# Gathering the tokens of four experts at a time in a decoder layer's mixture of experts

## The reference

```python
logits = (t @ w_router + b_router).astype(jnp.float32)
top_v, top_i = lax.top_k(logits, TOP_K)
gates = jax.nn.softmax(top_v, axis=-1)
...
gu = xb @ w_gate_up[ei] + b_gate_up[ei]
gate = jnp.minimum(gu[:, :D_FF], SWIGLU_LIMIT)
up = jnp.clip(gu[:, D_FF:], -SWIGLU_LIMIT, SWIGLU_LIMIT)
act = gate * jax.nn.sigmoid(gate * SWIGLU_ALPHA)
return ((up + 1.0) * act) @ w_down[ei] + b_down[ei]
```

## Time and profile before

| what | us |
|---|---|
| median of 3 runs | 1342.67 |
| lowest and highest of them | 1340.54, 1344.32 |
| profiled execution, its time | 1343.27 |
| span of the profiled execution | 1341.4 |
| PE busy in it (94%) | 1260.1 |
| DVE, ACT busy | 315.5, 159.9 |

### The profile page before, as it was taken

How to read it: one execution, slowest core, us unless ns; L and a number is a source line. 1 busy time by engine, 2 the same in 40 slices (tenths; PEclk the granted TensorE clock), 3 DMA queues, 4 the chain that set the end, 5 groups by cost and what they waited for, 6 DMA issues and landing times.

```text
span 1341.4 us, 15435 instructions
## 1 busy us (share of the span) xinstructions
PE 1260.1 (94%) x6339; PEld 606.3 (45%) x6339; DVE 315.5 (24%) x591; ACT 159.9 (12%) x305; POOL 84.5 (6%) x110
## 2 busy tenths in 40 slices
PE   5999999999799999999999999999999999999986
PEld 4757666764533434343443434343443434343431
DVE  2334446442211111122111111121111111121112
ACT  2214322112100001010000001010000001010001
POOL 4176500000000000000000000000000000000000
PEclk9989999989599999999999999999999999999998
DMA  9247570345386999999999999999999999999991
GB/s 316 79 131 245 170 250 1 139 196 184 157 322 260 414 421 414 419 417 417 419 414 422 414 422 414 419 417 417 419 415 422 414 422 414 419 417 417 420 414 43
DMA packets 92203, 447.63 MB, mean 334 GB/s; under 512 B 6282, under 2 KB 15926, under 8 KB 59269
## 3 DMA queue, kind: packets, MB, share of 16 engines
q1 hardware_dynamic: 85495, 427.36, 79.2%
q0 software_dynamic: 5632, 18.88, 4.5%
q10 hardware_dynamic: 1046, 0.97, 0.3%
HBM read 445.74 MB, written 1.68 MB: 334 GB/s over the span
## 4 chain that ended last, share of the span: by engine, by line
PE 76%; DMA 17%; DVE 3%; ACT 2%; issue 1%; SPq 1%; ACTq 0%; DVEq 0%
PE ps L942 19%; PE ps L997 17%; DMA arena<-in_w_gate_up 16%; PE ps L900 11%; PE ps L776 5%; PE ps L749 2%; PE ps L1009 2%; PE ps L605 2%; DVE arena L1642 2%; PE ps L1018 1%; PE ps L492 1%; PE ps L623 1%; PE ps L1014 1%; PE ps L538 1%; PE ps L646 1%
## 5 line engine op out<-in xcount | busy, mean ns | idle before, releaser
L942 PE MATMUL ps<-arena 128*64 128x512 f32 x2048 | 452.5, 597 | 30.8 <-DMA arena<-in_w_gate_up 23.6
L942 PEld LDWEIGHTS ps<-arena 128*64 128x64 f32 x2048 | 155.9, 137 | 315.2 <-issue 314.8
L997 PE MATMUL ps<-arena 128*64 128x512 f32 x1024 | 225.2, 597 | 4.8 <-ACT arena L1043 4.8
L1043 ACT ACTIVATE arena<-ps 128x512 f32<-128x512 f32 (+9 forms) x170 | 96.0, 582 | 532.2 <-PE ps L997 210.8
L900 PE MATMUL ps<-arena 128*128 128x128 f32 (+1 forms) x768 | 142.7, 318 | 1.3 <-DVE arena L1601 1.3
L997 PEld LDWEIGHTS ps<-arena 128*64 128x64 f32 x1024 | 74.4, 138 | 145.1 <-issue 144.6
L900 PEld LDWEIGHTS ps<-arena 128*128 128x128 f32 (+1 forms) x768 | 109.0, 195 | 44.2 <-issue 15.5
L1622 DVE TENSOR_SCALAR arena<-ps 128x512 f32<-128x512 f32 x32 | 22.1, 691 | 420.2 <-PE ps L942 420.2
L1217 ACT ACTIVATE arena<-arena 128x512 f32<-128x512 f32 x32 | 20.2, 630 | 490.1 <-DVE arena L1622 490.1
L1639 DVE TENSOR_TENSOR arena<-arena,ps 64x512 f32<-64x512 f32 x16 | 10.9, 679 | 270.0 <-PE ps L1014 270.0
L776 PE MATMUL ps<-arena 128*128 128x280 f32 x256 | 66.0, 414 | 0.0
(11 more groups left out here) (286 smaller groups left out, 765.9 us busy)
## 6 DMA issues: line engine op xcount, KB each, us to landing
arena<-in_w_gate_up SPq DMA_DIRECT2D x128, 2048.0 KB, 15.5
arena<-in_w_down SPq DMA_DIRECT2D x64, 2048.0 KB, 16.9
arena<-in_w_in SPq DMA_DIRECT2D x8, 1024.0 KB, 9.4
arena<-in_w_out SPq DMA_DIRECT2D x2, 2048.0 KB, 11.7
arena<-in_w_in SPq DMA_DIRECT2D x2, 1088.0 KB, 12.9
arena<-in_w_in SPq DMA_DIRECT2D x1, 2048.0 KB, 23.5
arena<-in_consts SPq DMA_DIRECT2D x1, 1104.0 KB, 8.8
arena<-in_w_uq SPq DMA_DIRECT2D x1, 768.0 KB, 15.8
```

What stands on the lines that cost most here:

```text
L942: m = mm(ps[SL * e:SL * e + SL, b, :], xg[:, 2 * c + kk, SL * e:SL * e + SL], w[e][:, kk, b, :], start=(c == 0 and kk == 0), stop=(c == 3 ...
L997: m = mm(ps[SL * e:SL * e + SL, u, :], hidT[:, 4 * c + kk, SL * e:SL * e + SL], w[e][:, kk, u, :], start=(c == 0 and kk == 0), stop=(c == ...
L1043: return act.activation(out, in_, ACT.Copy)
```

## The change

- `pick` is made for four experts at once (u = 4), once for every two pairs; `xg` holds the gathered rows of four experts (2048 columns in place of 1024). `pick`, `xg` and `pick_bias` change places in the arena.
- Pairs are now even (u = 0) or odd (u = 1). From pair 1 on, PE gathers only in odd pairs, for the two pairs that follow: `gather_four(0)` for the first four blocks of features where `gather` stood, and `gather_four(4)` for the other four behind the transposes of `hid`. Each is 12 matmuls with 256 columns and fills banks 6 and 7; between them ACT copies the banks out (`take_four`). Even pairs have no gather. Pair 0 still gathers for pair 1 alone, with 128 columns.
- `pickg` is still made for each pair (`weigh_pair`); the choice of four runs on DVE early in an even pair, once at the start, and at the end of pair 0.
- The loop's body is two pairs and runs 6 times (pairs 2 to 13); pairs 0, 1, 14 and 15 are written out. SP's code is untouched. In `pair`, the inner index u is renamed v; these lines are left out below.

```diff
@@ -196,16 +197,16 @@
         gates = at(take(NT * NE), NT * NE).rearrange("p (t e) -> p t e", t=NT)
         most = at(take(2), 2)
         most_i = at(take(2), 2).bitcast(I32)
-        pick = at(take(NT * P), NT * P).rearrange("p (t u s) -> p t u s", t=NT, u=2)
+        pick = at(norm2_start + SLOT, NT * 2 * P).rearrange("p (t u s) -> p t u s", t=NT, u=4)
         pickg = at(take(NT * P), NT * P).rearrange("p (t u s) -> p t u s", t=NT, u=2)
         pickT = at(hT0 + 4 * D, NT * P).rearrange("p (t n) -> p t n", t=NT)
-        xg = at(norm2_start + SLOT, KD * P).rearrange("p (k s) -> p k s", k=KD)
+        xg = at(take(KD * 2 * P), KD * 2 * P).rearrange("p (k s) -> p k s", k=KD)
         y_last = at(take(512), 512)[0:64, :]
...
-        pick_bias = at(take(P), P)
+        pick_bias = at(norm2_start + SLOT + 768, P)
         assert 4 * D + NT * P <= 2 * KD * T
...
@@ -891,21 +892,33 @@
 
             pe.sem_inc(pe_comb, 1)
 
-            def gather(count):
+            def gather(count, u):
 
                 pe.wait_ge(pick_ready, count)
                 for k in range(KD):
                     for t in range(NT):
                         n = ROWS[t]
                         m = mm(ps[:, 6 + k // 4, P * (k % 4):P * (k % 4) + P], h2[0:n, t, P * k:P * k + P],
+                               pick[0:n, t, u:u + 2, :].rearrange("p u s -> p (u s)"), start=(t == 0),
+                               stop=(t == NT - 1))
+                m.then_inc(pe_gather, 1)
+
+            def gather_four(k0):
+
+                for k in range(4):
+                    for t in range(NT):
+                        n = ROWS[t]
+                        m = mm(ps[:, 6 + k // 2, 2 * P * (k % 2):2 * P * (k % 2) + 2 * P],
+                               h2[0:n, t, P * (k0 + k):P * (k0 + k) + P],
                                pick[0:n, t, :, :].rearrange("p u s -> p (u s)"), start=(t == 0), stop=(t == NT - 1))
                 m.then_inc(pe_gather, 1)
 
-            def pair(n, extra, ahead, first=False, last=False):
+            def pair(n, extra, ahead, u=0, first=False, last=False):
+
                 if extra:
                     pe.wait_ge(y_added, 3 * n + 1)
-                    gather(n + 1)
-                pe.wait_ge(xg_ready, n + 1)
+                    gather(n - NP + NQ + 1, 0)
+                pe.wait_ge(xg_ready, n + 1 if first or extra or u else n + 2)
 
                 pe.wait_ge(pickg_ready, n + 1)
                 for t in range(NT):
...
                              [(kk, b) for kk in range(2) for b in range(4)])
                     for j, (kk, b) in enumerate(order):
                         for e in range(2):
...
-                            m = mm(ps[SL * e:SL * e + SL, b, :], xg[:, 2 * c + kk, SL * e:SL * e + SL],
+                            m = mm(ps[SL * e:SL * e + SL, b, :], xg[:, 2 * c + kk, P * u + SL * e:P * u + SL * e + SL],
...
+                elif ahead is not None:
+                    pe.wait_ge(pickT_ready, n + 1)
+                    pe.wait_ge(y_added, 3 * n + 1)
+                    pe.wait_ge(pick_ready, ahead)
+                    gather_four(0)
 
...
+                    pe.wait_ge(xg_ready, n + 2)
+                    gather_four(4)
                 for c in range(2):
...
-                    m = mm(ps[32 * u:32 * u + 32, 6, :], pickT[:, 2, 0:32], ye[:, 512 * u:512 * u + 512],
+                if first:
+                    pe.wait_ge(xg_ready, n + 2)
+                elif ahead is not None:
+                    pe.wait_ge(xg_ready, n + 3)
+                for v in range(2):
...
-            with pe.Fori(1, NP - 1) as p:
-                pair(p, False, True)
-            pair(NP - 1, False, False, last=True)
+            gather(1, 0)
+            pair(0, False, None, 0, first=True)
+            pair(1, False, 2, 1)
+            with pe.Fori(1, NQ - 1) as q:
+                pair(2 * q, False, None, 0)
+                pair(2 * q + 1, False, q + 2, 1)
+            pair(NP - 2, False, None, 0)
+            pair(NP - 1, False, None, 1, last=True)
             pe.wait_ge(most_ready, 1)
             count = pe.value_load(most_i[0:1, 0:1], min_val=0, max_val=T)
             with pe.If(count > SL):
...
 
 
-            def take_gathered(count):
+            def take_gathered(count, u):
                 act.wait_ge(pe_gather, count)
-                copy(xg, ps[:, 6:8, :].rearrange("p b (k s) -> p (b k) s", k=4)).then_inc(xg_ready, 1)
...
-
-            def pair(n, extra, ahead, first=False):
+                copy(xg[:, :, P * u:P * u + P], ps[:, 6:8, :].rearrange("p b (k s) -> p (b k) s", k=4)
+                     ).then_inc(xg_ready, 1)
+
+            def take_four(count, k0):
+                act.wait_ge(pe_gather, count)
+                copy(xg[:, k0:k0 + 4, :], ps[:, 6:8, :].rearrange("p b (k s) -> p (b k) s", k=2)).then_inc(xg_ready, 1)
+
+            def pair(n, extra, ahead, u=0, first=False):
...
                     act.activation(sgm[:, half_row], gate[:, half_row], ACT.Sigmoid, scale=ALPHA
                                    ).then_inc(sgm_ready, 1)
+                if ahead and u:
+                    take_four(n + 2, 0)
                 act.wait_ge(pe_hidT, 2 * n + 1)
                 copy(hidT[:, 0:4, :], ps[:, 4, :].rearrange("p (j n) -> p j n", j=4)).then_inc(hidT_act, 1)
-                if ahead:
-                    take_gathered(n + 2)
-                for u in range(2):
-                    if u == 0:
+                if first:
+                    take_gathered(n + 2, 1)
+                elif ahead and u:
+                    take_four(n + 3, 4)
+                for v in range(2):
...
-            def choose(experts, count, first):
-
-                iota = const["iota"][:, first].unsqueeze(1).unsqueeze(1).to_broadcast([P, NT, 2, SL])
-                dve.tensor_tensor(pick, iota, rank[:, :, experts].unsqueeze(3).to_broadcast([P, NT, 2, SL]),
+            def choose(experts, count, first, u=slice(0, 4)):
+
+                m = u.stop - u.start
+                iota = const["iota"][:, first].unsqueeze(1).unsqueeze(1).to_broadcast([P, NT, m, SL])
+                dve.tensor_tensor(pick[:, :, u, :], iota, rank[:, :, experts].unsqueeze(3).to_broadcast([P, NT, m, SL]),
                                   ALU.is_equal).then_inc(pick_ready, 1)
+
+            def weigh_pair(experts, count, u):
+
                 dve.wait_ge(pick_ready, count)
-                dve.tensor_tensor(pickg, pick, gates[:, :, experts].unsqueeze(3).to_broadcast([P, NT, 2, SL]),
+                dve.tensor_tensor(pickg, pick[:, :, u, :], gates[:, :, experts].unsqueeze(3).to_broadcast([P, NT, 2, SL]),
                                   ALU.mult).then_inc(pickg_ready, 1)
 
-            def pair(p, n, extra, first, ahead):
-                if ahead:
-                    dve.wait_ge(pe_gather, n + 1)
-                    dve.wait_ge(pe_pick, n + 1)
-                    choose(bass.ds(2 * p + 2, 2), n + 2, first)
+            def pair(p, n, extra, first, u, q=None, ahead=True):
+
                 if extra:
                     choose_bias(bass.ds(p, 1))
-                    choose(bass.ds(2 * p, 2), n + 1, first)
-
-                for u in range(2):
-                    at_u = slice(512 * u, 512 * u + 512)
-                    if u == 0:
+                    choose(bass.ds(2 * p, 2), n, first, slice(0, 2))
+                    weigh_pair(bass.ds(2 * p, 2), n - NP + NQ + 1, slice(0, 2))
+                elif u == 0:
+                    dve.wait_ge(pe_pick, n + 1)
+                    weigh_pair(bass.ds(2 * p + 2, 2), 1 if q is None else q + 1, slice(2, 4))
+                    if ahead and q is not None:
+                        dve.wait_ge(pe_gather, n + 2)
+                        dve.wait_ge(pickg_ready, n + 2)
+                        choose(bass.ds(2 * p + 4, 4), q + 2, first)
+                elif ahead:
+                    dve.wait_ge(pe_pick, n + 1)
+                    weigh_pair(bass.ds(2 * p + 2, 2), 2 if q is None else q + 2, slice(0, 2))
+
...
+                    dve.wait_ge(up_ready, 4 * n + 2 * v + 2)
+                    dve.wait_ge(sgm_ready, 2 * n + v + 1)
                     dve.tensor_tensor(hid[:, at_u], up[:, at_u], sgm[:, at_u], ALU.mult).then_inc(hid_ready, 1)
...
+                if u == 0 and q is None and not extra:
+                    dve.wait_ge(pe_gather, 2)
+                    choose(slice(4, 8), 2, first)
                 dve.wait_ge(y_added, 3 * n + 3)
...
-            choose(slice(0, 2), 1, slice(0, SL))
+            choose(slice(0, 4), 1, slice(0, SL))
+            weigh_pair(slice(0, 2), 1, slice(0, 2))
...
-            with dve.Fori(0, NP - 1) as p:
-                pair(p, p, False, slice(0, SL), True)
-            pair(NP - 1, NP - 1, False, slice(0, SL), False)
+            pair(0, 0, False, slice(0, SL), 0)
+            pair(1, 1, False, slice(0, SL), 1)
+            with dve.Fori(1, NQ - 1) as q:
+                pair(2 * q, 2 * q, False, slice(0, SL), 0, q)
```

(43 more changed lines are left out.)

47 lines of the change are left out of this document (23 added, 24 removed).

## The result

| | median us | lowest, highest |
|---|---|---|
| before, 5 runs | 1342.67 | 1339.18, 1344.32 |
| changed, 5 runs | 1356.71 | 1355.46, 1362.60 |

The change makes the kernel slower: ratio 1.013, 95% interval 1.0106 to 1.0153, some 14 us. That lies above the forecast's range, which ended at 1350 us. The profiled execution took 1362.6 us, the longest of its five, with a span of 1360.8 us against 1341.4.

What follows compares the result with a forecast made beforehand. The prediction took the loads (DMA) as the bound from pair 2 on, at 60.24 us a pair. 1343.27 + 0.6 for the start + 0 for the end gave 1343.9 us, no change, with range 1340.8 to 1350 us.

Steps and rivals of the forecast that it cites:

- The loads are the bound from pair 2 on: From pair 2 on, loads set 60.24 us a pair; PE has 1.69 us of air, so saving PE work gains nothing.
- Even pairs gain 6.35 us: Even pairs 2 to 14: dropping the 8.51 us gather saves PE 6.35 us, as making `hid` is then exposed.
- Odd pairs: 10.7 us for the wide gather, 11.7 at most: Odd pairs 1 to 13: 48 instructions of 256 columns at 0.222 us, making PE 2.2 us late (2.0 to 3.2).
- The cover is 3.7 us, 2.9 for pair 2: Queued transfers at the queue's thinnest place, said to absorb the odd pair's 2.2 us delay at cost 0.
- The start: +0.6 us: Ahead of the first gather: DVE's choice for 768 elements, not 384, delays it unhidden by 0 to 0.6 us.
- Rival 1: PE falls to half clock behind longer waits in odd pairs; no change, or 1355 us in the longer form; chance 0.11.
- Rival 2: Wide gather: 256 columns cost twice 128 (17.0 us), delaying seven odd pairs; +33 us, 1377 us; chance 0.03.
- Rival 3: The two-pair loop body no longer stays on the core, so PE stands at each turn; 1359 us; chance 0.05.
- Rival 4: In the loop, loads were held back by PE, so 53 us would go, to 1290 us; chance 0.03.

Runs made afterwards that it cites:

- e10: The kernel before, with the third token tile at 128 rows only in the gathers of pairs 1 to 14: 1341.42 us, ratio 0.9999.
- e1: The changed kernel, with the third token tile taken at all 128 rows (zero-padded) in the wide gather: 1346.99 us, ratio 1.0037.
- e3: The changed kernel without the third token tile in the wide gather, so 24 tokens are left out: 1341.34 us, ratio 1.0008.
- e7: The changed kernel, with 128 rows in the wide gather's third tile and a discarded narrow gather in the even pairs: 1343.82 us, ratio 1.0017.
- e2: The changed kernel, with the wide gather's second half moved into the following even pair, ahead of its third gate stage: 1346.16 us, ratio 1.0031.
- e5: The changed kernel, with the wide gather's second half moved into the even pair and 128 rows in the third tile in all gathers: 1331.68 us, ratio 0.9923.
- e6: The kernel before, with 128 rows in the third token tile in all its gathers: 1329.47 us, ratio 0.9905.
- e11: The kernel before, with 128 rows in the third tile only in the first gather and that of pair 0: 1328.93 us, ratio 0.9900.
- e9: The changed kernel, with the wide gather's tiles taken 0, 1, 2 and 2, 1, 0 in turn, the third keeping 24 rows: 1352.34 us, ratio 1.0083.

## Why the prediction was wrong

- *The loads are the bound from pair 2 on.* Right: in e10 41 us less work on TensorE left the time as it was.
- *Even pairs gain 6.35 us.* Right: at 641 us of the changed kernel the transposes wait for `hid` as those of pair 15 did:

```profile
641.40 0.65 PE L983 MATMUL ps<-arena 128*128 128x128 f32 x4 [0.96 <-DVE arena L1674]
643.28 0.66 PE L983 MATMUL ps<-arena 128*128 128x128 f32 x4 [1.23 <-DVE arena L1683]
643.87 7.09 PE L1018 MATMUL ps<-arena 128*64 128x512 f32 x32
```

- *Odd pairs: 10.7 us for the wide gather, 11.7 at most.* **This is the step that failed.** It took 13.5 us, and the odd pair was 4.8 us late, not 2.2, more than the 3.7 us queued. The term left out 16 changes between 128 and 24 rows at 0.17 to 0.20 us, together 2.9 us (13.5 against 10.6 in e1). The rows of 280 columns were nearest in columns but not in rows; with equal tiles they were right to 0.002 us (e1: 0.220 against 0.222 scaled). Rows ahead of the prediction held the hint: 8.51/48 = 0.177 us for 128 columns, where half of the 0.218 us that the down stages give for 256 columns is 0.109. I divided and did not ask where 0.07 us went.
- *The cover is 3.7 us, 2.9 for pair 2.* Right for the loop: at full clock, delays of -1.4 us (e3) and 2.1 (e7) gave no gap there, 4.8 us (changed kernel) gave 0.8 to 1.4. Too large for pair 2: the gap in pair 1 is 0.4 to 0.5 us at a delay of 2.1 (e1, e7) and 2.6 at 4.8, so the cover there was 1.6 to 2.2 us. The delay of 4.8 us was 2.6 more than the 2.2 of the text, of which the gather's term is 2.8; since the cover stood there as a threshold, that was enough to cross it. Below it a delay costs nothing, above it the excess, and more with half clock, in each odd pair.
- *The start: +0.6 us.* It was 0.4: the choice takes 0.95 us, and the first gather's wait is 1.73 us, not 1.33.

```profile
347.26 1.01 PE L901 MATMUL ps<-arena 128*128 128x128 f32 x3 [1.73 <-DVE arena L1642]
```

- *Rival 1, half clock behind longer waits.* It happened, mostly in the short form of 3.4 us, where I had given the whole rival 0.11. Its price was computed on a delay of 2.2 us; e1 against e7 gives 3.2 us for about that, not the 1.2 of the text, with intervals that overlap. The even pairs' waits for `hid`, behind which half clock came too, the text did not count. On the true delay the gaps behind a slow last gate stage were 2.0 to 4.0 us, the others in the loop 0.8 to 1.4.
- *Rival 2, no saving*: false in this form (0.281 us is 1.6 times 0.177, not twice), but it was the right place. *Rival 3, the loop's body*: five packets of instructions between 520 and 1290 us, against one, while a body of two pairs turned six times; no refetch at each turn.

```profile
q8 instruction: 5, 0.08, 0.1%
```

- *Rival 4*: false; no kernel moved more than 418 GB/s in the loop.

Open: how much of the changed kernel's loss is half clock on top of the delay; why half clock follows one wait and not the next of the same length; and why e2, without a gap, is 3.6 us above before (2.2 from its first gather on). e5's median is 2.2 us above e6's, with intervals that overlap. In the traces most of it is the last pair: from the first down stage to the scatter behind it e5 takes 1309.48 - 1284.55 = 24.93 us and e6 1305.18 - 1284.85 = 20.33, because in e5 that down stage fell on half clock:

```profile
1284.55 10.09 PE L1020 MATMUL ps<-arena 128*64 128x512 f32 x32 [0.84 <-DMA arena<-in_w_down]
```

## What to carry to other kernels

Where one queue is saturated, ask two things of every edit: whether its gain lies ahead of the saturated stretch, where a microsecond is a microsecond, or in it, where it is nothing; and whether any delay exceeds what is queued at the thinnest place, which the shortest landing less the landing into an empty queue gave within the loop, though not at its start. Price an instruction from rows that match it in every dimension, rows of the stationary operand included, and account for any difference between its time and the same columns elsewhere. Padding a short tile to the full 128 rows was worth 1% here, all of it ahead of the saturated stretch (e11), and it was a smaller edit than the one under study.

## What the runs showed of the hardware

- Loading stationary operands of 128 and 24 rows in turn costs TensorE 0.17 to 0.20 us a change at full clock, at 256 columns (e1, e9, changed kernel); in the narrow gather of 128 columns padding saves (8.44 - 5.46)/16 = 0.19 us a change (e6).
- A first gather of 128 columns with such changes stayed at 1.2 GHz for its whole 15 us (before, e10); with equal rows the clock rose to 2.4 GHz 5 to 6 us after its start (e11, e6).
- Waits of 2.1 to 2.9 us for loads were often followed by 3.4 us at 1.2 GHz, though not always (2.85 us at 816.96 and 1186.54 us of the changed kernel). Waits of up to 1.9 us in the kernel before and up to 2.0 in e7 were not. Four stretches in the changed kernel began behind two waits of only 0.8 to 1.5 us each, close together. The Trainium skill, "TensorE: Matmul & The Clock Gate", section "HAM oscillation", tells of half clock behind waits of 3 to 5 us for loads; the shorter ones measured here were enough to be followed by it.
